# Queries and keys of eight attention heads computed in a first stage of their own, with seven block products in place of eight

## What is computed

```python
h = rmsnorm(x, norm_w)
proj = h @ w_in                                   # 2048 x 6400
qa, ka, va, ga, qb, kb, vb, gb = split(proj)      # 1024 each; kb, vb 128 each
qa, ka = rope(rmsnorm(qa, q_norm_a)), rope(rmsnorm(ka, k_norm_a))   # per group of 64
# A: 8 heads, two causal softmax maps per head
a = softmax(q0 k0' / 8) - lam * softmax(q1 k1' / 8)
ya = rmsnorm(a @ va, subln_w) * (1 - lam_init) * silu(ga)
# B: 16 query heads on 2 key/value heads, window 128, learned sinks
yb = banded_attention(qb, kb, vb, sinks) * silu(gb)
out = x + concat(ya, yb) @ w_out                  # 2048 x 2048
```

## Time and profile before

| | busy us | share | instructions |
|---|---|---|---|
| TensorE | 1807.0 | 96% | 8920 |
| VectorE | 1109.2 | 59% | 2255 |
| ScalarE | 799.8 | 43% | 2116 |
| GpSimd | 439.0 | 23% | 664 |

### The profile page before, as it was taken

How to read it: one execution, slowest core, us unless ns; L and a number is a source line. 1 busy time by engine, 2 the same in 40 slices (tenths; PEclk the granted TensorE clock), 3 DMA queues, 4 the chain that set the end, 5 groups by cost and what they waited for, 6 DMA issues and landing times.

```text
span 1877.2 us, 27880 instructions
## 1 busy us (share of the span) xinstructions
PE 1807.0 (96%) x8920; PEld 1507.0 (80%) x8920; DVE 1109.2 (59%) x2255; ACT 799.8 (43%) x2116; POOL 439.0 (23%) x664
## 2 busy tenths in 40 slices
PE   3899999999999999999999999999999889999999
PEld 3788878888788887888878888888888678788887
DVE  5734465665656657566575666758677866333333
ACT  5411354444544445444444444445444554222221
POOL 6512131322313223131231312313223521000000
PEclk9999999999999999999999999999999889999999
DMA  5122222222222222222222222323323544444445
GB/s 201 36 79 73 84 72 78 78 78 78 71 77 77 77 78 71 85 69 87 68 74 86 73 84 74 105 82 83 109 80 98 189 127 122 162 154 161 142 143 177
DMA packets 256504, 184.97 MB, mean 99 GB/s; under 512 B 31136, under 2 KB 227744, under 8 KB 255392
## 3 DMA queue, kind: packets, MB, share of 16 engines
q1 hardware_dynamic: 254352, 183.85, 32.3%
q10 hardware_dynamic: 2064, 0.01, 0.1%
HBM read 138.71 MB, written 45.09 MB: 98 GB/s over the span
## 4 chain that ended last, share of the span: by engine, by line
PE 79%; DVE 9%; issue 4%; DMA 3%; ACT 2%; POOL 2%; SPq 1%; DVEq 0%; ACTq 0%
PE ps_a L854 19%; PE ps_a L856 19%; PE ps_a L855 19%; PE ps_b L938 3%; PE ps_b L856 3%; PE ps_b L854 3%; PE ps_b L855 3%; PE ps_a L898 2%; DVE stage_rows L1124 2%; DMA qkv_sb<-qkv_a_dram 2%; PE ps_a L897 2%; PE ps_b L953 2%; PE ps_b L891 2%; PE ps_b L984 1%; DVE w_lo_sb L1124 1%
## 5 line engine op out<-in xcount | busy, mean ns | idle before, releaser
L854 PE MATMUL ps_a<-hT_hi,w_hi_sb 128*128 128x512 f32 x1696 | 694.1, 409 | 7.2 <-DVE stage_rows L1208 4.5
L856 PE MATMUL ps_a<-hT_hi,w_lo_sb 128*128 128x512 f32 x1696 | 667.4, 394 | 0.0
L855 PE MATMUL ps_a<-hT_lo,w_hi_sb 128*128 128x512 f32 x1696 | 664.1, 392 | 0.0
L1124 DVE TENSOR_TENSOR w_lo_sb<-w_raw_sb,w_hi_sb 128x512 fp32r<-128x512 f32 (+1 forms) x320 | 228.3, 716 | 272.1 <-ACT w_hi_sb L657 270.1
L856 PEld LDWEIGHTS ps_a<-hT_hi,w_lo_sb 128*128 128x128 f32 x1696 | 320.1, 189 | 71.8
L854 PEld LDWEIGHTS ps_a<-hT_hi,w_hi_sb 128*128 128x128 f32 x1696 | 321.2, 189 | 70.2 <-issue 7.2
L855 PEld LDWEIGHTS ps_a<-hT_lo,w_hi_sb 128*128 128x128 f32 x1696 | 321.8, 190 | 58.5
L657 ACT ACTIVATE w_hi_sb<-w_raw_sb 128x512 fp32r<-128x512 f32 (+1 forms) x320 | 197.8, 620 | 226.4 <-DMA w_raw_sb<-in_w_out 95.0
L817 ACT ACTIVATE expd<-ps_a,neg_max 128x256 f32<-128x256 f32 (+7 forms) x128 | 95.1, 743 | 213.3 <-DVE neg_max L1265 211.4
L749 ACT ACTIVATE attention_parts<-ps_b 128x512 fp32r<-128x512 f32 (+3 forms) x160 | 76.9, 521 | 224.2 <-PE ps_b L938 224.0
L1124 DVE TENSOR_TENSOR ps_a<-ps_a,mask 128x128 f32<-128x128 f32 (+2 forms) x192 | 77.5, 417 | 142.2 <-PE ps_a L898 140.8
(11 more groups left out here) (126 smaller groups left out, 2651.6 us busy)
## 6 DMA issues: line engine op xcount, KB each, us to landing
w_raw_sb<-in_w_in SPq DMA_DIRECT2D x200, 256.0 KB, 3.1
w_raw_sb<-in_w_out SPq DMA_DIRECT2D x104, 256.0 KB, 3.1
qkv_a_dram<-stage_rows SPq DMA_DIRECT2D x48, 256.0 KB, 2.4
qkv_sb<-qkv_a_dram SPq DMA_DIRECT2D x64, 192.0 KB, 3.0
x_raw_sb<-in_x SPq DMA_DIRECT2D x8, 1024.0 KB, 7.6
gates_dram<-stage_rows SPq DMA_DIRECT2D x32, 256.0 KB, 2.7
gate_y<-gates_dram SPq DMA_DIRECT2D x128, 64.0 KB, 2.4
y_dram<-gate_y SPq DMA_DIRECT2D x128, 64.0 KB, 2.3
```

Of the source, the lines that this page charges most:

```text
L854: pe.matmul(dst, a_hi, b_hi, start=start, stop=False)
L855: pe.matmul(dst, a_hi, b_lo, start=False, stop=False)
L856: return pe.matmul(dst, a_lo, b_hi, start=False, stop=stop)
L1124: return dve.tensor_tensor(o, a, b, op)
```

## The change

Queries and keys of the eight A heads leave the passes. They are computed in a first stage, as one 1024 x 2048 by 2048 x 2048 product.

- The product is cut into 2 x 2 blocks (tokens, depth, and q columns against k columns), and computed with seven block products in place of eight. The operands and results are sums of blocks. With a1, b1, a2, b2 the four blocks of the normalised x, the seven stationary operands come from `z_src`, the moving ones (sums of blocks of w_in) from `load_tile`.
- Tokens are the rows of the output here: the normalised, transposed x is stationary and 512 columns of weights move. A tile j (of 112) is a 128-row block of depth: 12 matmuls into four PSUM banks, 16 tiles for each product, two groups of eight.
- For products 2 to 5 (`TWO_LOADS`) the moving operand is a sum of two loads, formed on GpSimd (`combine_w`); products 2 and 3 store it to DRAM and 3 and 4 load such sums. The stationary sums are formed on GpSimd (`sum_h`) and split on ScalarE and VectorE (`z_high`, `z_low`).
- Results leave PSUM by ScalarE (`copy_group`) and VectorE (`add_part`), partly summed on GpSimd (`add_row`). Each of 32 row tiles of 128 tokens x 512 columns is squared, summed, normalised and rotated (`square_row`, `sum_row`, `row_norm`, `scale_row`, `turn_row`) by tables that already hold the norm weights (`parameters`), and stored (`store_row`).
- Dates are given by the tile j: `EVAC_*`, `ROW_AT`, `H_SPLIT`, `z_unit`. Each engine has a `first_stage(j)` that runs for j in 0 to 111 and goes on beside the two key/value tiles.
- The normalised x goes to DRAM (`store_h`) and comes back (`load_h`) at the end of the stage, to be split into hT_hi and hT_lo for the other projections.
- The start loads four row blocks of x and begins the first product when 512 tokens are transposed; the other four blocks are transposed after tiles 0, 2, 4 and 6.
- Beside an A unit there are now two tiles, v and gate: 16 slots of one half each (`place`), so 12 matmuls per slot. Passes with B tiles are as before.
- Before the first pass TensorE waits, as before, for k_zeros; GpSimd's two memsets now wait for all parked rows to be stored.

The core of the diff:

```diff
-NQ_IN = 4 * (2 + 4 * (AH + BC))
+NQ_IN = 4 * (2 + 2 * AH + 4 * BC)
+def place(k, s):
+    if k == "A":
+        return s // 8, s % 8 // 2, (s % 2,)
+    return s // 4, s % 4, (0, 1)
...
+NK = KT // 2
+NOP = 7
+NT = NOP * 2 * NK
+SETS = 4
+TWO_LOADS = (2, 3, 4, 5)
+EVAC_BB = {24 + 2 * n: n for n in range(8)}
+EVAC_V = {56 + 8 * c + r: 4 * c + r for c in range(2) for r in range(4)}
+EVAC_BT = {72 + 2 * n: n for n in range(8)}
+EVAC_H = {88 + 8 * c + r: 4 * c + r for c in range(2) for r in range(4)}
+EVAC_SB = {104 + 8 * c + r: 4 * c + r for c in range(2) for r in range(4)}
+ROW_START = ([25 + 2 * n for n in range(8)] + [74 + 2 * n for n in range(8)] + [92 + 2 * n for n in range(8)]
+             + [110 + 2 * n for n in range(8)])
+H_SPLIT = {t: k for k, t in enumerate((85, 86, 87, 88, 97, 98, 99, 100, 101, 102, 103, 104, 112, 113, 114, 115))}
...
@@ TensorE
                     if d:
-                        quarter(d, u, s % 4, 0, before)
+                        q, halves = place(d["kind"], s)[1:]
+                        for b in halves[:1]:
+                            quarter(d, u, q, b, before)
...
+            def product_tile(j):
+                g, k, op = j // NK, j % NK, j // 16
...
+                elif k == 0 and g >= 2:
+                    by, n = evacs_before(g - 2)
+                    pe.wait_ge(sm["ev_" + by], n)
+                pe.wait_ge(sm["f_lo"], j + 1)
...
+                for r in range(4):
+                    t = slice(k * 512 + r * P, k * 512 + (r + 1) * P)
+                    mm = three((ps_a, ps_b)[g % 2][:, r, :], z_hi[op % 2][:, t], z_lo[op % 2][:, t],
+                               w_hi[:, j % 4, :], w_lo[:, j % 4, :], k == 0, k == NK - 1)
+                mm.then_inc(sm["f_used"], 1)
...
@@ ScalarE
+            def first_stage(j):
+                if j + 2 < NT:
+                    tile_hi(j + 2)
...
+                if z_unit(j):
+                    z_high(*z_unit(j))
+                if j - 2 in ROW_AT:
+                    scale_row(ROW_AT[j - 2])
+                if j in ROW_AT:
+                    square_row(ROW_AT[j])
+                if j in H_SPLIT:
+                    h_high(H_SPLIT[j])
...
@@ VectorE
+            def first_stage(j):
+                if j + 2 < NT:
+                    tile_lo(j + 2)
...
+                evacuate(j)
+                if z_unit(j):
+                    z_low(*z_unit(j))
+                if j - 3 in ROW_AT:
+                    turn_row(ROW_AT[j - 3])
+                if j - 1 in ROW_AT:
+                    sum_row(ROW_AT[j - 1])
+                if j in H_SPLIT:
+                    h_low(H_SPLIT[j])
...
@@ GpSimd
+            def first_stage(j):
+                if j + 3 < NT and (j + 3) // 16 in TWO_LOADS:
+                    combine_w(j + 3)
+                if j - 1 in EVAC_BT:
+                    add_row(EVAC_BT[j - 1])
+                if j - 1 in EVAC_H:
+                    add_row(8 + EVAC_H[j - 1])
+                if j - 1 in ROW_AT:
+                    row_norm(ROW_AT[j - 1])
+                if j in H_SPLIT:
+                    h_low(H_SPLIT[j])
...
@@ SyncE
+            def first_stage(j):
+                if j + 2 < NT and (j + 2) // 16 in (2, 3):
+                    store_comb(j + 2)
+                if j - 4 in ROW_AT:
+                    store_row(ROW_AT[j - 4])
+                if j + SETS < NT:
+                    load_tile(j + SETS)
```

More of the change, by code:

```diff
@@ L1171, in _ @@
-            parts.append(left)
-            magic = 1.5 * 2.0 ** 23
-            turns = o_sb[:, :]
-            for table, quarter_turn in ((cos_t, 0.25), (sin_t, 0.0)):
+            for r in range(4):
+                if r < 3:
+                    scale_x(r + 1)
+                weigh_x(r, 0)
+                if r == 3:
+                    z_low(0, 0)
+                    z_low(0, 1)
+                weigh_x(r, 1)
+                if r == 3:
+                    z_low(0, 2)
+                    z_low(0, 3)
+                weigh_x(r, 2)
+                if r in (1, 2):
+                    tile_lo(r - 1)
@@ L1384, in body @@
                         y_out(back2, it, first)
[L1385 removed]
+                    if d and last_step(first, s) and not d["turned"]:
                         gate(d, 0)
@@ L1483, in norms @@
+            for n in range(16):
+                sum_h(n)
+            for j in range(NT):
+                first_stage(j)
             def norms(d, b):
```

708 lines of the change are left out of this document (535 added, 173 removed).

## The result

The changed kernel takes 2054.3 us (median of four runs, 2053.9 to 2057.1) where the kernel before takes 1877.55 (median of four). The ratio is 1.094, with a 95% interval of 1.093 to 1.096. The prediction said slower, by 30 us; it is 177. The time of 2054.3 lies far above the range of 1880 to 1936.

A forecast was written before the change was run, and what follows sets the result against it. TensorE's matmuls were taken to bound the seven passes. Start 34, products 305.8, transposes 6, stalls 25, key/value tiles 43.7 + 0.9, first A projection 43.7 + 1.8, passes 576.1 gave 1037.0 against 1007.5, hence 1907 us, range 1880 to 1936.

The forecast's parts named there:

- TensorE's sum: Whole kernel: 349.4 us of matmuls and 14.1 of turn_tile removed, 305.8 added, so 57.7 us less TensorE work.
- the passes: Seven A passes: 82.6 us each, first 80.5, with 12.7 stall per pass waiting for lo_qk; 576.1 against 811.5.
- The first stage: The 112 product tiles: 2.73 us of TensorE each, 305.8 in all, plus stalls from VectorE, GpSimd and loads.
- Sum 25, bounds 3 and 50: First-stage stalls: 17 in rounds 77 to 92, 4 in 28 to 43, 2 from 93 on, 2 for k_zeros.
- Rival 3: Between c1 and next c0 in the passes: the step's chain does not show, 89 us less stall, 1818; chance 0.11.
- Rival 4: TensorE's granted clock falls from 2.4 to 1.2 GHz after short stalls in the passes: 1990; chance 0.05.
- What was said to queue behind lo_qk: In the passes, split_w on VectorE and SyncE's load of the next step come later but stay covered, cost nothing.
- The start: Before the first product: norm_c lands at 14.4, first tile at 29.3; effective start 34, bounds 30 to 40.
- with its waits 57: 2: Rounds 93 on of the first stage: VectorE 50 of 54.6 us, with its waits 57, so stall 2.
- The loads' chain: Rounds 28 to 43: turn_row, store_row, load, combine_w, tile_hi, tile_lo take 6.3 us where VectorE leaves 5.8; stall 4.
- Predicted stall 17: Rounds 77 to 92: VectorE and GpSimd exclude each other, 67.9 us in 43.7; lead of two tiles covers 5.5.
- Rival 2: First stage: late turn_row holds SyncE's weight loads, late row_norm holds ScalarE's tile_hi; stall 50, 1932; chance 0.14.

The follow-up runs named there:

- The reordering: Changed kernel with ScalarE squaring row R+1 before scaling row R, and VectorE summing row R+1 before turning row R: 2001.5 us.
- SyncE's order: On the kernel with rows reordered (2001.5), SyncE issues each tile's load ahead of the store of a row: 1990.4 us.
- the kernel with the quarters first: On the kernel with all earlier edits and the norm taken from GpSimd (1955.8), SyncE's key/value quarter loads go ahead of row stores: 1945.4 us.
- the earlier memsets: On the 1945.4 kernel, GpSimd's two k_zeros memsets wait only for the eight rows parked in their place, not all sixteen: 1939.3 us.

## Why the prediction was right or wrong

**Direction right, size wrong by 147 us.** TensorE's sum, the passes and the rest hold. The step that failed is "The first stage": its "Sum 25, bounds 3 and 50" added up each engine's work and two short chains, and put the waits from row to row at nothing. Measured, the stretch up to the first pass takes 156 us more than the sum with that 25 in it. Of this the rows' loop, taken away alone, gives back 53: it is the largest single cause found, and a third of the miss.

**The passes: right.** Predicted 82.6 each and 80.5 for the first, 576.1 in all. Measured 74.5, 83.3, 81.6, 81.6, 81.6, 84.5 and 83.2, 570.4. The predicted stall was 12.7 for each pass, with 0.5, 1.6, 1.6 and 1.0 us behind steps 0 to 3 (5.5 - 5.0, 5.1 - 3.5, 5.4 - 3.8, 5.6 - 4.6) and 2.5 behind step 7. TensorE's waits for lo_qk in one pass of the changed kernel, first in sum and then the first five:

```profile
PE ps_a L1235 <- DVE attention_parts L1474: 11.2, 8, 2.4
...
782.81 0.32 PE L1235 MATMUL ps_a<-attention_parts,q_hi_lo 128*128 128x128 f32 x1 [2.44 <-DVE attention_parts L1474]
792.37 0.38 PE L1235 MATMUL ps_a<-attention_parts,q_hi_lo 128*128 128x256 f32 x1 [0.32 <-DVE attention_parts L1474]
800.61 0.43 PE L1235 MATMUL ps_a<-attention_parts,q_hi_lo 128*128 128x384 f32 x1 [1.35 <-DVE attention_parts L1474]
809.39 0.49 PE L1235 MATMUL ps_a<-attention_parts,q_hi_lo 128*128 128x512 f32 x1 [1.36 <-DVE attention_parts L1474]
818.76 0.49 PE L1235 MATMUL ps_a<-attention_parts,q_hi_lo 128*128 128x512 f32 x1 [0.91 <-DVE attention_parts L1474]
```

The wait ahead of step 0 is the one behind step 7: 2.44 for 2.5, then 0.32 for 0.5, 1.35 for 1.6, 1.36 for 1.6, 0.91 for 1.0. The eight are all of TensorE's idle time in the pass. So the chain read off, where TensorE never waited for it, was the chain that bound once its cover was halved. Rival 3 is out. Rival 4 is out for the passes: the clock is 0.96 to 1.00 there, in spite of these waits. Its mechanism did act where the prediction didn't look, in the first stage, at 0.82 to 0.88 in the stretches with longer waits: there the stalls were priced as waits only, and the slower matmuls behind them were left out. What was said to queue behind lo_qk at no cost did cost nothing. Only the first pass is off, 74.5 for 80.5.

**The start: the bound was reached, not the value.** The first product began at 34.1, not 29.3, and tile 8 at 68.6 in place of 61.6. The first work that had waited for norm_c began at 17.6, not 14.4, and the transposes of the fifth block of x, 3.6 us, began at 40.8, not 36.

**Tiles 8 to 23: missed altogether.** The prediction has no line for the tables and for twelve sums of h, since each is small where it stands. What was not asked is when GpSimd may begin them: the store of each sixteenth of h goes out in one SyncE round, so the last one sets the block's time, and in it VectorE had its six table operations. 15.6 us in one stop, 2.6 in the slow tile behind it, 20.3 in the stretch.

**Tiles 32 to 47, 96 to 111 and the key/value part: the loop.** The prediction summed the work of each engine and found room (VectorE 50 of 54.6, "with its waits 57: 2"). The reordering shows that the same work in another order gives 12, 20 and 10 us back there. The failed step is that a chain was followed for the loads (turn_row, store_row, load, combine_w, tile_hi, tile_lo, priced at 4 us), but not for the rows, although of its larger steps only the price of ScalarE's eight scalings was missing. One turn takes 7.55 against 5.46, and there are 32 rows: 67 us by estimate, if every one of them shows, of which the reordering gave 53 back. The loads' chain was real: SyncE's order gave 11 us back where 4 stood in the sum.

**Tiles 80 to 95: the right mechanism, mis-sized.** Predicted stall 17, measured 42. Some 14 of the difference are the two loops (86.0 falls to 71.7 with both gone). The other 11 go to the term of exclusion, by a sum and not by a run of its own. GpSimd's sum of two SBUF tensors was taken as 1.73 - 0.69 = 1.04 us; where VectorE is idle it takes 1.28:

```profile
237.79 1.28 POOL L1976 TENSOR_TENSOR w_sets_sb<-w_sets_sb 128x512 f32<-128x512 f32 x1 [1.73 <-DMA w_sets_sb<-w_comb_dram]
...
L1474 DVE TENSOR_TENSOR w_lo_sb<-w_sets_sb,w_hi_sb 128x512 fp32r<-128x512 f32 x84 | 83.4, 997 | 98.0 <-ACT w_hi_sb L910 97.8
```

30 of them make 38.4, with VectorE's 36.7 that is 75, and 71 to 73 us is what these 16 tiles take in every kernel without the loops that keeps the sums. So of the 5.5 us of lead that the prediction took off, 2 to 4 at most counted. The sum is not tight: with 16 of the 30 cut to 8 columns it gives 55, and the run gave 61.9. VectorE's tile_lo, 0.69 alone, has a mean of 1.00 over the stage, so the expected sign ("well over 0.69") was there; GpSimd's combine came to 1.40 in the mean, not 1.7, and many ran where VectorE stood idle. The other sign, a busy share of VectorE over 0.9, did not show: it is 0.63 in tiles 80 to 95 and 0.56 in tiles 96 to 111. This alone says that the stage was not bound as the prediction had it. GpSimd's sum of 31.2 us also left out its three operations for each row, some 2.5 us or 20 for eight rows; GpSimd is busy 57 us in these tiles. The Trainium skill, page "SBUF — State Buffer", section "SBUF: two separate sides", has the two engines take the port pair as an exclusive lock for a whole instruction. Between two of GpSimd's 1024-column sums a VectorE operation of one column took 2.34 us, so the trace agrees. The prediction had weighed its letter against GpSimd's power of 128x8 and followed the trace, which the changed kernel bears out: a subtraction of two SBUF inputs ran undelayed inside such a power. Here the measurement goes against the page's letter, and it decides.

```profile
393.34 1.65 POOL L1938 TENSOR_TENSOR ss_rows<-row_mean,small 128x8 f32<-128x8 f32 x1
393.44 1.22 DVE L1474 TENSOR_TENSOR hT_lo<-h_b,hT_hi 128x1024 fp32r<-128x1024 f32 x1
```

**k_zeros: priced 2, cost 10.7.** The memsets do wait for the last row's store, and TensorE for them:

```profile
567.59 1.95 POOL L2072 MEMSET attention_parts<- 64x1024 f32 x2 [6.66 <-DMA qkv_a_dram<-g_sb]
...
569.59 0.80 PE L1186 MATMUL ps_a<-hT_hi,w_hi_sb 128*128 128x512 f32 x1 [10.66 <-POOL attention_parts L2072]
```

With the rows reordered it is 7.5, so the loop made 3 of it. In the kernel with the quarters first it is 5.8, and the earlier memsets gave 6.1 back.

**The rivals.** Rival 2 named the right kind, in-order queues in which a late turn_row holds the loads and a late row_norm holds tile_hi, and gave it 50 us as the whole stall of the stage. It was some 175. It was reasoned from engines that are late, not from a loop that makes them late at every row, and so had no size. The bounds were the mistake in judgement: nothing in the trace of before shows these queues at work, so those of an unseen pipeline had to be wider than 3 to 50.

## What to carry to other kernels

Where several engines work through a stream of items in fixed order, write down the order of each engine's queue for items R and R+1 and look for a loop: a path of inputs and queue orders that leads from a step of item R back to the same step of item R+1, as here from scale(R) over turn(R), sum(R+1) and norm(R+1) to scale(R+1), though item R+1 needs nothing of item R. Where it is longer than the time allowed for an item, as here 7.55 us against 5.46, it sets the pace however idle the engines are; here swapping two calls, on each of two engines, took it away. Price a stall by more than its wait, too: tile 23 took 5.3 us, not 2.7, behind a long one. A sum of busy times only gives a floor; with idle engines on every side and each waiting for the next, look for the loop first, and for exclusion only after it.
